# A hybrid mLSTM and GLA decoder step on one core: the first two decay levels of each gated head stand in window A

## The reference, cut to what matters

```
b = cumsum(lc)                       # within a chunk
decay = exp(where(mask, b_t - b_s, -inf))
A = einsum('td,sd,tsd->ts', qc, kc, decay)
o = A @ vc + (qc * exp(b)) @ S
S_new = exp(bL) * S + (kc * exp(bL - b))^T @ vc
```

## Time and profile before

| | |
|---|---|
| median of 3 runs | 1972.3 us (1971.16 to 1972.94) |
| the profiled execution's own time | 1975.96 us |
| span of its profile | 1974.2 us |
| mean granted TensorE clock | 0.983 |
| busy: TensorE, VectorE, GpSimd, ScalarE | 1912.5, 1049.3, 689.5, 680.2 us |

### The profile page before, as it was taken

One profiled execution on the slowest core, in us unless ns is written; L12 is line 12 of the kernel. 1 busy time (PEld: TensorE's weight loads), 2 busy tenths in 40 slices (PEclk: granted clock), 3 DMA queues, 4 the chain that ended last, 5 costly groups with the idle time before them and its releaser, 6 DMA issues.

```text
span 1974.2 us, 33248 instructions
## 1 busy us (share of the span) xinstructions
PE 1912.5 (97%) x13205; PEld 1823.1 (92%) x13205; DVE 1049.3 (53%) x1900; ACT 680.2 (34%) x1425; POOL 689.5 (35%) x582
## 2 busy tenths in 40 slices
PE   7899999999999999999999999899999999999997
PEld 4899999999999999999888999899999999999996
DVE  5730464402644116432164678876756666566656
ACT  4523334333333333332243554222232223222333
POOL 3211142311322213322132584334454345444441
PEclk8999999999999999999998999999999999999999
DMA  9241221412212322223241642111121112111212
GB/s 333 73 105 44 67 81 49 137 49 73 81 49 87 94 72 75 52 82 103 58 139 43 203 132 85 43 33 54 44 65 34 53 44 65 48 39 44 65 44 99
DMA packets 211266, 155.07 MB, mean 79 GB/s; under 512 B 10196, under 2 KB 195732, under 8 KB 210600
## 3 DMA queue, kind: packets, MB, share of 16 engines
q1 hardware_dynamic: 210810, 152.73, 26.1%
q10 hardware_dynamic: 302, 0.22, 0.0%
HBM read 131.42 MB, written 21.50 MB: 77 GB/s over the span
## 4 chain that ended last, share of the span: by engine, by line
PE 84%; DVE 6%; POOL 4%; issue 3%; ACT 2%; DMA 1%; SPq 0%; DVEq 0%; ACTq 0%; POOLq 0%
PE bank L913 37%; PE bank L2062 17%; PE bank L2031 11%; PE bank L1952 3%; PE bank L998 3%; POOL act_lo L2306 2%; PE bank L1016 1%; PE bank L1018 1%; PE bank L1021 1%; PE bank L949 1%; PE bank L1919 1%; PE bank L1059 1%; POOL w_lo L2272 1%; PE bank L936 1%; POOL f_lo L2272 1%
## 5 line engine op out<-in xcount | busy, mean ns | idle before, releaser
L1258 POOL TENSOR_TENSOR w_lo<-w_raw,w_hi 128x512 fp32r<-128x512 f32 x128 | 180.1, 1407 | 716.0 <-ACT w_hi L1081 716.0
L913 PE MATMUL bank<-h_hi,w_hi 128*128 128x352 f32 x1536 | 334.6, 340 | 1.4 <-ACT w_hi L1081 1.4
L913 PE MATMUL bank<-h_hi,w_lo 128*128 128x352 f32 x1536 | 314.9, 327 | 1.1 <-POOL w_lo L1258 1.1
L913 PE MATMUL bank<-h_lo,w_hi 128*128 128x352 f32 x1536 | 314.3, 327 | 0.0
L913 PEld LDWEIGHTS bank<-h_hi,w_hi 128*128 128x128 f32 x1536 | 256.1, 191 | 23.3 <-issue 18.7
L913 PEld LDWEIGHTS bank<-h_hi,w_lo 128*128 128x128 f32 x1536 | 261.7, 190 | 2.5 <-POOL w_lo L1258 2.5
L913 PEld LDWEIGHTS bank<-h_lo,w_hi 128*128 128x128 f32 x1536 | 261.9, 191 | 0.0
L2272 POOL TENSOR_TENSOR f_lo<-w_raw,f_hi 128x512 fp32r<-128x512 f32 x107 | 144.2, 1353 | 200.9 <-ACT f_hi L2100 200.9
L2272 POOL TENSOR_TENSOR w_lo<-w_raw,w_hi 128x512 fp32r<-128x512 f32 x107 | 145.4, 1364 | 156.6 <-ACT w_hi L2100 156.6
L2609 DVE SCALAR_TENSOR_TENSOR x_t<-bank,ada,x_t 128x352 f32<-128x352 f32 (+1 forms) x288 | 158.2, 569 | 58.7 <-PE bank L2031 41.3
L1081 ACT ACTIVATE w_hi<-w_raw 128x512 fp32r<-128x512 f32 x128 | 80.4, 628 | 134.8 <-PE bank L913 134.7
(11 more groups left out here) (480 smaller groups left out, 3819.5 us busy)
## 6 DMA issues: line engine op xcount, KB each, us to landing
w_raw<-in_w_in SPq DMA_DIRECT2D x128, 256.0 KB, 3.0
w_ada_tile<-in_w_ada SPq DMA_DIRECT2D x32, 512.0 KB, 4.3
w_raw<-in_w_out SPq DMA_DIRECT2D x48, 256.0 KB, 2.9
w_raw<-in_w_ffn_gate SPq DMA_DIRECT2D x44, 256.0 KB, 3.0
w_raw<-in_w_ffn_up SPq DMA_DIRECT2D x44, 256.0 KB, 3.0
w_raw<-in_w_ffn_down SPq DMA_DIRECT2D x44, 256.0 KB, 2.8
w_ada_ring<-in_w_ada SPq DMA_DIRECT2D x8, 1024.0 KB, 8.2
x_scratch<-x_turned_rows SPq DMA_DIRECT2D x1, 4224.0 KB, 14.1
```

The lines of the kernel that those rows point to most:

```text
L913: last = pe.matmul(g.ps[b][:, 0:n], x[:, s, k, :], y[:, 4 * h + k, c0:c0 + n], start=(h == 0 and k == 0 and m == 0), stop=(h == 1 and k == ...
L1258: pool.tensor_tensor(Wl[:, s], raw[:, r], Wh[:, s].bitcast(F32), ALU.subtract).then_inc(s_lo, 1)
```

## The change

Levels 0 and 1 of head i of mixer B leave windows B and L and stand in window A of the same head, in slots 42 and 46, `level0_k` and `level1_k` in 40 and 43. To make room, `samples0` and `samples1` move from 31 and 35 to 27 and 29, `alpha` from 37 to 31, `sums` from 45 to 36, in front of `norm` (39), and `vt1` from 32 to 33. In L the other levels spread: 2 to 7 in slots 1, 3, 5, 7, 9, 11 (before 4, 5, 7, 9, 10, 11). The condition tiles and a few small stages move by some slots in every window. SyncE's load of the mix waits for `level2` instead of `level1`. Two code lines follow from the move: GpSimd looks up in which window the level before stands, and the product on q names mixer B's buffer, since in window A `q` is mixer A's.

```
     "A": [("decay", 1), ("ada_load0", 2), ("scores", 6), ("keys", 6), ("interq", 8),
-          ("ada0", 9), ("masked", 12), ("ada_load1", 12), ("chunk0", 13), ... ("vt0", 14), ("chunk3", 15),
-          ... ("adas0", 24), ("ada_load2", 24), ("samples0", 31), ("vt1", 32), ("ada2", 33), ("samples1", 35),
-          ("ada_load3", 36), ("gate0", 36), ("alpha", 37), ("norm", 39),
-          ("ada3", 42), ("turn0", 44), ("adas1", 45), ("sums", 45), ("gate1", 47), ("turn1", 47)],
+          ("masked", 12), ("ada0", 13), ("chunk0", 13), ... ("ada_load1", 13), ("vt0", 15), ("chunk3", 15),
+          ... ("adas0", 23), ("ada_load2", 24), ("samples0", 27), ("samples1", 29), ("ada2", 31), ("alpha", 31),
+          ("ada_load3", 32), ("vt1", 33), ("gate0", 36), ("sums", 36), ("norm", 39),
+          ("level0_k", 40), ("ada3", 42), ("level0", 42), ("level1_k", 43), ("turn0", 44), ("adas1", 46),
+          ("level1", 46), ("gate1", 47), ("turn1", 47)],
-    "B": [("level0_k", 1), ("ada_load0", 3), ("level0", 3), ("level1", 5), ("conv_q", 7), ("taps_q", 8), ("level2", 10),
-          ... ("ada0", 12) ... ("vt0", 17) ... ("ada1", 24) ... ("ada2", 36), ("ada_load3", 39) ... ("ada3", 45), ("turn0", 46), ("adas1", 46)
+    "B": [("ada_load0", 3), ("conv_q", 7), ("taps_q", 8), ("level2", 10),
+          ... ("ada0", 14) ... ("vt0", 16) ... ("ada1", 22) ... ("ada2", 35), ("ada_load3", 36) ... ("ada3", 46), ("turn0", 46), ("adas1", 47)
-    "L": [("level0_k", 1), ("ada_load0", 2), ("level0", 2), ("level1_k", 2), ("level1", 3), ("level2", 4), ("level3", 5),
-          ("level4_k", 5), ("ada0", 6), ("level4", 7), ("ada_load1", 8), ("level5", 9), ("gate_r0", 9), ("level6", 10),
-          ("level7", 11), ("ada1", 12), ("keys", 12), ...
+    "L": [("level2", 1), ("ada_load0", 2), ("level3_k", 2), ("level3", 3), ("level4", 5), ("ada0", 5), ("gate_r0", 6),
+          ("level5", 7), ("ada_load1", 8), ("level6_k", 8), ("level6", 9), ("level7", 11), ("ada1", 11), ("keys", 12), ...

+def level_window(w, l):
+    return "A" if f"level{l}" in [n for n, _ in AT_SLOT["A"]] else w

-                    elif x[0] == "level1" and w == "L":
-                        wait_use(sp, w, i, USE[w]["level1"])
+                    elif x[0] == "level2" and w == "L":
+                        wait_use(sp, w, i, USE[w]["level2"])

-                            wait_use(pool, w, i, USE[w][f"level{l - 1}"] + USES[f"level{l - 1}"] - 1)
+                            wl = level_window(w, l - 1)
+                            wait_use(pool, wl, i, USE[wl][f"level{l - 1}"] + USES[f"level{l - 1}"] - 1)

-                            dve.tensor_tensor(halves(QD[:, 0:top], l, 1), halves(q[:, 0:top], l, 1), halves(TB[:, 0:top], l, 1),
+                            dve.tensor_tensor(halves(QD[:, 0:top], l, 1), halves(Q[1][:, 0:top], l, 1), halves(TB[:, 0:top], l, 1),
```

More of the change, by code:

```diff
@@ L523 @@
           ("conv_k", 23), ("taps_k", 24), ("silu_k", 25), ("decay_load", 25), ("interq_load", 25), ("vt1", 29)],
-    "A": [("decay", 1), ("ada_load0", 2), ("scores", 6), ("keys", 6), ("interq", 8), ("ada0", 9),
[7 rows of a table removed]
+    "A": [("decay", 1), ("ada_load0", 2), ("scores", 6), ("keys", 6), ("interq", 8),
[7 rows of a table added]
           ("silu_k", 30), ("masked", 30), ("keys", 30), ("chunk0", 31), ("chunk1", 31), ("chunk2", 32), ("chunk3", 32),
[3 rows of a table removed]
[3 rows of a table added]
           ("turn1", 47)],
[2 rows of a table removed]
[2 rows of a table added]
           ("keys", 12), ("masked", 13), ("chunk0", 13), ("chunk1", 13), ("adas0", 14), ("ada_load2", 14), ("chunk2", 14), ("gate0", 14),
```

## The result

The changed kernel took 1992.6 us, the median of four runs (1988.6 to 1993.8), where the kernel before took 1971.7: a ratio of 1.0102, 95% interval 1.0085 to 1.0119, so 21 us slower. The forecast was slower too, but 1978.6 us with a range up to 1988. The profiled execution took 1992.94 us with a span of 1991.2; beside the 1974.2 of the profiled execution before, 17.0 us have to be found in the two traces.

What follows compares the result with a forecast made beforehand. TensorE, busy 1912.5 of 1974.2 us, was taken as the bound. Terms -12.3 - 0.6 + 10.8 + 3.6 + 4.8 = +6.3 us gave 1982.3 profiled, 1978.6 as median; range 1966 to 1988.

Steps and rivals of the forecast that it cites:

- Window L: First 12 slots of window L: spreading the levels closes nearly all gaps, gaining 12.3 us (bounds 9 and 14.3).
- ada0: Condition tile in window L: its load lands behind the mix's load, so TensorE idles 0 to 2.2 us, taken as 0.6.
- Rival 4: Window L: the mix's load delays ada0 by 2.2 us or more and the clock falls; 1981.8 us, 0.50 jointly with forecast.
- the 14.3: Microseconds lost in window L's first 12 slots before the change: 8.1 idle, about 4.5 lower clock, the rest at gap edges.
- The chain before level 0: Window A, slots 36 to 42: VectorE and ScalarE queues make TensorE idle 2.7 us in each of four heads, 10.8 us.
- Rival 1: Window A: products avoid GpSimd, so level 0 waits 0.7 us a head and no clock falls; 1965.8 us, chance 0.20.
- Level 1: Window A, slot 46: adas1's addition precedes its product on q in VectorE's queue; 0.9 us idle, 3.6 in four heads.
- Windows B: Levels leaving windows B give back 0.6 of the first stretch's 1.2 us of TensorE idle time (bounds 0 and 1.2).
- The clock: Behind level 0 of window A: three clock falls in four heads at 1.6 us, 4.8 us; none behind level 1, alpha's unchanged.
- rival 3: Window A: two clock falls in a row behind each level 0, as at 1055 us; +14.7 us, 1987.0, chance 0.09.
- the pair of falls at 1055 us: Window L before the change: two clock falls in a row, the model for 3.3 us a head behind level 0.
- Rival 2: Window A: idle as forecast but the clock holds and one or two of alpha's falls vanish; 1971.4 us, chance 0.21.

## Why the prediction was right in kind and wrong in size

- *Window L.* Forecast 12.3 us of gain, measured 11.9. Level 2 idles 1.07 us (forecast 0.8), level 5 0.67 (0.6). ada0 did not wait at all (0.6), although the load of the mix was issued ahead of its tile and landed after 9.1 us. Rival 4 is out. The forecast's 4.5 us for the lower clock in L are 5.05 by its own rows, which shifts what is left to the edges and leaves the 14.3 as they are.
- *The chain before level 0.* Right in every step, and short by 0.5 us: 3.24 us idle against 2.7. In head 0 slot 35 ends at 215.25 and its gate_t activation, the second of the pair at 215.50, at 216.35, 1.1 us later where the forecast took 0.6. From 212.73 on ScalarE's queue in front of the pair had no gap: a table load of 1.28 us behind alpha's logarithm, a gate_t activation, and vt1's copies, now in slot 33. No run separates these. 4 x 0.54 = 2.2 us. Rival 1 is out: GpSimd was met in both places.
- *Level 1.* Forecast 0.9, measured 0.87.
- *Windows B.* The forecast gave back 0.6 us of the 1.2 us of idle time in the first stretch. The trace before has 0.65 of it there, in front of level 2 of the three heads. The changed kernel has 0.07 left at level 2, but 0.43 new at level 5 and 0.22 at level 6, so windows B cost 1.5 us more instead of 0.6 less.
- *The clock.* This is the step that failed, as the size of a term. The forecast put "three falls in four heads at 1.6 us, 4.8 us" and left alpha's. Measured in the profile: two falls in a row in all four heads (13.8 us, 12.9 without what lay in the idle time), one of 1.7 behind level 1 in three heads (5.1), alpha's 6.9 gone: 11.1 us net in place of 4.8. The fall behind level 1, which the forecast put at none, is 5.1 of it. The double fall was rival 3 with a chance of 0.09. The argument against it was that the pair of falls at 1055 us had an earlier fall in front of it, which the runs showed to be no condition: some 3.2 us of idle time between ada3 and a level came with two in a row in ten heads of twelve and with one in the others, 1.14 us at nearly the same place with none or one. Rival 3's own time, 1987.0, is still too low, as it has no fall behind level 1. Rival 2 is out: no head kept the full clock behind level 0.
- *The base.* The sum was made against a profiled execution with all four of alpha's falls, 3.7 us above the median, and then carried over to the median. By the traces the change costs 17.0 us, by the medians 20.8; the three profiles of the kernel before span 6.8 us mostly by falls that come and go.

With the measured terms the sum is 16.4 idle in A + 1.5 in B - 11.9 + 11.1 = 17.1 us, against 17.0. The forecast's +6.3 lacks 2.0 of idle time in A, 6.3 of the clock, 0.4 of L's gain and 2.1 in windows B.

## What to carry to other kernels

An operation that moves into a region where the main engine never waits has to be checked against the queues of the helpers, not against their busy shares: lay out what stands in front of its operand on every engine, with the places where two engines meet, and compare with the main engine's arrival. Here three pieces' worth of time was too little for a chain of six steps, and moving any one stage of it, the gate product, the norm or the level itself, took 23 to 31 us off. Price an idle time of about 3 us among light matmuls together with the clock behind it, which here doubled it. The 1.14 us cost itself and a fall of 1.7 us in two heads of four; 0.87 us cost only itself where no longer idle time stood in front. And look for new waits wherever the moved work is now missing, too: the helpers meet at other moments there, as in windows B.

## What the runs showed of the hardware that was not expected

The lower clock doesn't answer to a kernel's order alone. With the same instructions, alpha (2.1 us of matmuls with 16 rows) was followed by the lower clock in four heads of one execution and in one head of two others. Only the long idle time before level 0 came with it always, in twelve heads of twelve. The start-to-start distance of heads in the kernel before differs by it: 256.1 us with a fall behind each alpha, 254.5 us without. And the falls can begin while TensorE still stands idle: in the changed kernel's profile that was so in heads 1 to 3.
